# Two blocks of a transformer layer: the matrix that picks a head's decay sums written out by GpSimd, and a second add of squares

## The chip, the cores and the metric

One Trainium2 chip, one core. The time is microseconds on the device for one run of the whole program. The program's engines are TensorE (PE; its weight loads are shown apart as PEld), VectorE (DVE), ScalarE (ACT), GpSimd (POOL) and SyncE (SP), which issues the DMAs.

## The reference

Two blocks work on 256 tokens of width 1024 in float32. The first is a mixer of attention and a recurrence, then a mixture of 32 experts; each ends in a layer norm. The second, where the change lies, is a mixer with a Mamba-2 scan, then a gated MLP. Of that mixer what matters is this, cut down:

```python
u = rmsnorm(h, norm_mix_w)
gate_a, gate_s, b_a, c_a, v_a, z, xbc, dt_raw = split(u @ w_in)
y_a = (b_a * causal_dwconv(c_a * v_a, conv_a_w)) @ w_a_out
xs, bs, cs = split(silu(causal_dwconv(xbc, ssd_conv_w) + ssd_conv_b))
dt = softplus(dt_raw + dt_bias)
a_cum = cumsum(dt * -exp(a_log))
decay_in = exp(where(causal, a_cum[l] - a_cum[s], -inf))
y = (C_l . B_s * decay_in[l, s]) @ (xs * dt) + ...
yf = (y + d_skip * xs) * silu(z)
yf = yf * rsqrt(mean(yf * yf over a group of 512) + EPS) * ssd_norm_w
out = (sigmoid(gate_a) * y_a + sigmoid(gate_s) * (yf @ w_s_out)) @ w_o
```

There are 32 heads of 64 and 4 groups of 8 heads. a_cum is kept for each head and token, and each head needs its own row of 256 sums on all 128 partitions.

## The kernel before

The program is one list of instructions for each engine, in the order in which the code writes them; semaphores hold them together. `mixer2` (L1506) holds the lists of the second block's mixer: `sync`, `gpsimd`, `scalar`, `vector`, `tensor`. It follows the experts, whose last work is a layer norm of the two token tiles; that norm's last DVE instruction (L227) raises `s.h_ready` to 1 and then 2.

**Products.** Activations lie with features on partitions and 256 tokens along the row. The weights come in units of 1024x256, numbered 0 to 55. Each float32 factor is split in a high part, rounded to F32R, and a low part, so that one product becomes three (L167 to L169, high by high, low by high, high by low). A unit is 48 such products of 256 columns. For each unit SP loads 1 MB into one of three slots, ACT rounds it (L111) and DVE takes the difference (L115); TensorE runs the unit when that is done and its PSUM bank has been read.

**The start of the mixer.** When h is normed, ACT sums its squares, TensorE scales and transposes h in one step (L1947), ACT rounds the result to `u_hi` (L1658), and DVE makes `u_lo` from it (L1787, eight instructions of 256 columns, one operand in PSUM and one in SBUF). DVE's list runs L227, L115 for unit 0, L1782 (half of a norm's weights), L1784 (`w_dt_lo`, the low part of the step widths' weights, both operands in SBUF), the eight L1787, then L115 for units 1 and 2. TensorE's unit 0 waits before each group of three products for its piece of `u_lo`. After unit 0 come 24 small products with `w_dt`, then units 1, 2 and so on.

**The scan.** Units 24 to 27 also make the sums: `acum`, 64 rows by 256 tokens, holds for each of 32 heads the high part and, 32 rows below, the low part of its sums. `pick` is a matrix of 64x32 with a one at rows h and 32 + h of column h: DVE writes it (L1887) as the sum of two pieces of the identity. From unit 28 on, each unit goes with two heads: `row_sums` (L1985) multiplies a column of `pick`, read with a step of zero as a 64x128 matrix, with `acum`, which puts the head's sums on all partitions; ACT makes the decay from it, DVE weighs it (L1863), and `scan_out` (L1995, L1996) multiplies it with the tokens.

```python
out, head = s.bank[3 + p % 2][:, T * hh:T * hh + T], pick[:, h:h + 1].to_broadcast([2 * N_HEADS, P])
m = pe.matmul(out, lhsT=head, rhs=acum[:, :], start=True, stop=True)
```

**The squares.** When the four blocks of a group are done, POOL multiplies them with the gate (L1635), ACT squares them in two pieces of 128x512 (L1715), POOL adds the two (L1638) and so leaves two blocks of 256 tokens, and TensorE sums over partitions and blocks with a constant matrix (`mean_squares`, L2007, float32, two passes for each block). ACT makes the root and POOL scales (L1641). For groups 0, 1 and 2 this stands in TensorE's list behind units 35, 38 and 42, each time ahead of a `scan_out`. Group 3 has no add on POOL and takes four products.

Of the kernel before, what the change touches and what calls it, by code (L numbers as in the profile page):

```python
# [10 lines left out]
F32R = mybir.dt.float32r  # L11
# [5 lines left out]
P = 128  # L17
T = 256
# [1487 lines left out]
def mixer2(nc, A, s):  # L1506

    XBC_TAPS, A_TAPS, N_HEADS, N_GROUPS = 4, 3, 32, 4
    with ExitStack() as ctx:
        def sb(name, shape, dt=FP32):  # L1510
            return ctx.enter_context(nc.sbuf_tensor(name, shape, dt))
# [3 lines left out]
        def sem(name):  # L1515
            sems.append(nc.alloc_semaphore(name))
            return sems[-1]
# [12 lines left out]
        squares = [bcv[:, 6:8, :].rearrange("p a t -> p (a t)"), sb("squares", [P, 2 * T])[:, :]]  # L1530
# [5 lines left out]
        shift = sb("decay_shift", [P, 3, N_HEADS])  # L1536

        acum = sb("acum_hi_lo", [2 * N_HEADS, T], F32R)
        pick = sb("pick_head", [2 * N_HEADS, N_HEADS], F32R)
        rstd = sb("group_rstd", [P, T])  # L1540
        half_w = sb("half_norm_w", [P, 16])

        C = lambda name: s.con[:, SHARED.index(name), :]
# [13 lines left out]
            "cb_mm", "cbm_ready", "xt_mm", "xtok_ready", "row_mm", "decay_ready", "m_ready", "y_mm", "y_ready", "z_tanh",  # L1557
            "gated", "squared", "ms_mm", "rstd_ready", "normed", "y_hi", "y_done"))
        w_dt_split, dt_heads_mm, dt_copied = sem("m3_w_dt_split"), sem("m3_dt_heads_mm"), sem("m3_dt_copied")
        squares_added = sem("m3_squares_added")  # L1560
        merged, merged_hi, merged_done, out_first, h_done = (sem("m3_" + n) for n in (
            "merged", "merged_hi", "merged_done", "out_first", "h_done"))
        s.h_done = h_done
# [52 lines left out]
                st.load(sp, n // 3, n % 3, unit(n), 4, 512)  # L1616

        def gpsimd(pool):
            pool.wait_ge(evac_sem[2], 4)
            pool.wait_ge(evac_sem[1], 4)  # L1620
            pool.wait_ge(evac_sem[0], 4)
            for j in range(4):
                c = pair(bcv, 4 + j)
                pool.tensor_tensor(c, c, pair(bcv, 8 + j), ALU.mult).then_inc(cv_ready, 1)
            for j in range(4):
                pool.wait_ge(conv_a, j + 1)
                pool.wait_ge(cv_ready, 4)
                pool.tensor_tensor(pair(bcv, j), pair(bcv, j), pair(bcv, 8 + j), ALU.mult).then_inc(ya_ready, 1)

            for g in range(N_GROUPS):  # L1630
                y = xbc[:, 4 * g:4 * g + 4, :].rearrange("p a t -> p (a t)")
                pool.wait_ge(y_ready, 4 * g + 4)
                pool.wait_ge(evac_sem[(33 + 2 * g) % 3], use_of[33 + 2 * g] + 1)
                pool.wait_ge(evac_sem[(32 + 2 * g) % 3], use_of[32 + 2 * g] + 1)
                pool.tensor_tensor(y, y, zt[:, 4 * g:4 * g + 4, :].rearrange("p a t -> p (a t)"), ALU.mult).then_inc(gated, 1)  # L1635
                if g < N_GROUPS - 1:
                    pool.wait_ge(squared, 2 * g + 2)
                    pool.tensor_tensor(squares[0], squares[0], squares[1], ALU.add).then_inc(squares_added, 1)  # L1638
                pool.wait_ge(rstd_ready, g + 1)
                pool.wait_ge(gated, g + 1)  # L1640
                pool.tensor_tensor(xbc[:, 4 * g:4 * g + 4, :], xbc[:, 4 * g:4 * g + 4, :],  # L1641
                                   rstd[:, :].unsqueeze(1).to_broadcast([P, 4, T]), ALU.mult).then_inc(normed, 1)
# [134 lines left out]
        def vector(dve):  # L1777
            own = Count(dve, dve_own)
            step = own.add
# [99 lines left out]
            for n in range(24, 44):  # L1879
                if n == 24:  # L1880
                    ya_low(3)
                if n == 25:
                    for g in range(4):
                        masked_cb(g)
                    dve.wait_ge(shift_ready, 1)
                    lo = slice(N_HEADS, 2 * N_HEADS)
                    step(dve.tensor_tensor(pick[:, :], C("identity")[0:2 * N_HEADS, 0:N_HEADS], C("identity")[0:2 * N_HEADS, lo], ALU.add))  # L1887
                    own.wait()
                    dve.tensor_tensor(acum[lo, :], s.bank[7][lo, P:P + T], acum[lo, :].bitcast(FP32), ALU.subtract).then_inc(shift_ready, 1)
                if n in (26, 27):  # L1890
                    for f in range(4):
# [47 lines left out]
        def tensor(pe):  # L1939
# [38 lines left out]
            def row_sums(p):  # L1978

                if p >= 2:  # L1980
                    pe.wait_ge(decay_ready, p - 1)
                for hh in range(2):
                    h = 2 * p + hh
                    out, head = s.bank[3 + p % 2][:, T * hh:T * hh + T], pick[:, h:h + 1].to_broadcast([2 * N_HEADS, P])
                    m = pe.matmul(out, lhsT=head, rhs=acum[:, :], start=True, stop=True)  # L1985
                m.then_inc(row_mm, 1)

# [10 lines left out]

            def mean_squares(g):
                if g < N_GROUPS - 1:  # L2000
                    parts = 2
                    pe.wait_ge(squares_added, g + 1)
                else:
                    parts = 4
                    pe.wait_ge(squared, 2 * g + 2)
                for i in range(parts):
                    m = pe.matmul(s.bank[7][:, 0:T], lhsT=C("mean512"), rhs=squares[i // 2][:, T * (i % 2):T * (i % 2) + T], start=(i == 0), stop=(i == parts - 1))  # L2007
                m.then_inc(ms_mm, 1)
# [27 lines left out]
                        m.then_inc(xt_mm, 1)  # L2036
            pe.wait_ge(xtok_ready, 5)
            pe.wait_ge(shift_ready, 2)
            row_sums(0)
            for n in range(28, 44):  # L2040
                if n == 28:
# [422 lines left out]
```

## Time and profile before

| | |
|---|---|
| median of 3 runs | 1716.53 us (1716.46 to 1716.59) |
| span of the profiled execution | 1714.0 us; its own time is not given apart from the runs |
| PE busy | 1660.5 us (97%) |
| DVE busy | 679.2 us (40%), 1188 instructions |
| ACT busy | 576.4 us (34%) |
| POOL busy | 43.3 us (3%), 26 instructions |
| HBM | 312 GB/s over the span |

Times in the trace are microseconds from the span's start. The busy share of TensorE is a sum over stages: in the experts (about 230 to 1140 us) it also waits for weights from HBM, in the second block (from 1140 us) it mostly does not. The granted clock of TensorE has two levels, 1.0 (2.4 GHz) and 0.5 (1.2 GHz). A record's length includes the time in which the instruction stood at its engine's door, so a longer record of the same form shows a hindrance and not more work.

### The profile page before, as it was taken

How to read it: one execution, taken by the hardware profiler on the slowest of the kernel's cores; microseconds unless marked ns; L12 is line 12 of the kernel's file. 1: busy time of each engine (PE TensorE's matmuls, PEld its weight loads, DVE VectorE, ACT ScalarE, POOL GpSimd, SP SyncE). 2: the span in 40 equal slices, each digit the busy share in tenths (PEclk: the TensorE clock that was granted, in tenths of full speed). 3: DMA queues.
4: the chain of work that ended last, by engine and by line, in shares of the span. 5: the costliest groups of instructions: out<-in, count | busy, mean ns of one | idle time of the engine just before them, and what ended most of it. 6: DMA issues, size and time to landing. Idle time of an engine off the chain costs nothing.

```text
span 1714.0 us, 24055 instructions
## 1 busy us (share of the span) xinstructions
PE 1660.5 (97%) x9963; PEld 1057.6 (62%) x9963; DVE 679.2 (40%) x1188; ACT 576.4 (34%) x818; POOL 43.3 (3%) x26
## 2 busy tenths in 40 slices
PE   8999999999999999999999999999999999999998
PEld 7999863333333333333333333349999999989996
DVE  4676651212121212121212121244597565666654
ACT  5653521111111111111111111144464687465433
POOL 0000000000000000000000000000100032000000
PEclk9999999999999999999999999999999999999999
DMA  8554999999999999999999999975555444555552
GB/s 265 197 191 130 346 391 414 425 430 430 429 431 430 430 429 433 427 432 429 431 430 431 430 430 429 430 262 175 182 181 174 143 141 136 173 184 175 190 188 86
DMA packets 150860, 535.09 MB, mean 312 GB/s; under 512 B 7890, under 2 KB 102510, under 8 KB 118030
## 3 DMA queue, kind: packets, MB, share of 16 engines
q1 hardware_dynamic: 150798, 534.20, 79.3%
q8 instruction: 46, 0.75, 0.2%
q14 instruction: 16, 0.13, 0.0%
HBM read 533.13 MB, written 1.05 MB: 312 GB/s over the span
## 4 chain that ended last, share of the span: by engine, by line
PE 61%; DMA 16%; DVE 1%; ACT 1%; issue 0%; SPq 0%; ACTq 0%
PE bank L1389 15%; PE bank L167 10%; PE bank L168 10%; PE bank L169 10%; PE bank L1405 8%; DMA expert_weights_late<-in_expert_w_up_dram 8%; DMA expert_weights<-in_expert_w_up_dram 8%; PE bank L1371 2%; PE bank L1352 2%; PE bank L1396 2%; PE bank L1360 1%; PE bank L1995 0%; PE bank L1365 0%; PE bank L1985 0%; ACT back_w_hi L111 0%
## 5 line engine op out<-in xcount | busy, mean ns | idle before, releaser
L1289 DVE TENSOR_TENSOR pre_act<-bank,bias_now 128x512 f32<-128x512 f32 x64 | 44.0, 687 | 657.4 <-PE bank L1396 657.4
L115 DVE TENSOR_TENSOR back_w_lo<-raw_weights,back_w_hi 128x2048 fp32r<-128x2048 f32 x90 | 205.6, 2286 | 92.2 <-ACT back_w_hi L111 91.1
L1389 PE MATMUL bank<-expert_weights_late,x_gathered 128*64 128x512 f32 x1024 | 226.6, 594 | 15.1 <-DMA expert_weights_late<-in_expert_w_up_dram 15.1
L111 ACT ACTIVATE back_w_hi<-raw_weights 128x2048 fp32r<-128x2048 f32 x90 | 170.1, 1891 | 95.5 <-PE bank L169 95.5
L167 PE MATMUL bank<-u_hi,back_w_hi 128*128 128x256 f32 x704 | 201.0, 285 | 0.0
L168 PE MATMUL bank<-u_lo,back_w_hi 128*128 128x256 f32 x704 | 199.1, 283 | 0.0
L169 PE MATMUL bank<-u_hi,back_w_lo 128*128 128x256 f32 x704 | 199.1, 283 | 0.0
L1389 PEld LDWEIGHTS bank<-expert_weights_late,x_gathered 128*64 128x64 f32 x1024 | 72.1, 137 | 166.3 <-issue 135.1
L1389 PE MATMUL bank<-expert_weights,x_gathered 128*64 128x512 f32 x736 | 163.6, 594 | 10.0 <-DMA expert_weights<-in_expert_w_up_dram 10.0
L1211 ACT ACTIVATE raw_weights<-bank 128x512 f32<-128x512 f32 x32 | 19.1, 597 | 399.9 <-PE bank L1389 399.9
L167 PEld LDWEIGHTS bank<-u_hi,back_w_hi 128*128 128x128 f32 x704 | 134.9, 192 | 2.1 <-issue 0.4
L169 PEld LDWEIGHTS bank<-u_hi,back_w_lo 128*128 128x128 f32 x704 | 135.0, 192 | 0.0
L168 PEld LDWEIGHTS bank<-u_lo,back_w_hi 128*128 128x128 f32 x704 | 135.0, 192 | 0.0
L1389 PEld LDWEIGHTS bank<-expert_weights,x_gathered 128*64 128x64 f32 x736 | 51.9, 137 | 117.6 <-issue 96.7
L1405 PE MATMUL bank<-expert_weights_late,activations 128*64 128x512 f32 x512 | 113.4, 595 | 0.2 <-DVE activations L1302 0.2
L167 PE MATMUL bank<-v_hi,back_w_hi 128*128 128x256 f32 x352 | 99.9, 284 | 0.2 <-DVE v_lo L2214 0.2
L168 PE MATMUL bank<-v_lo,back_w_hi 128*128 128x256 f32 x352 | 99.6, 283 | 0.0
L169 PE MATMUL bank<-v_hi,back_w_lo 128*128 128x256 f32 x352 | 99.6, 283 | 0.0
L1227 ACT ACTIVATE raw_weights<-bank 128x512 f32<-128x512 f32 x32 | 19.1, 597 | 207.9 <-PE bank L1405 207.9
L1405 PE MATMUL bank<-expert_weights,activations 128*64 128x512 f32 x384 | 85.5, 594 | 0.0
L167 PE MATMUL bank<-x_hi,m_w_hi 128*128 128x256 f32 x272 | 77.7, 286 | 0.0
L168 PE MATMUL bank<-x_lo,m_w_hi 128*128 128x256 f32 x272 | 76.8, 282 | 0.0
(412 smaller groups left out, 2656.7 us busy)
## 6 DMA issues: line engine op xcount, KB each, us to landing
expert_weights_late<-in_expert_w_up_dram SPq DMA_DIRECT2D x64, 2048.0 KB, 26.3
expert_weights<-in_expert_w_up_dram SPq DMA_DIRECT2D x46, 2048.0 KB, 26.3
expert_weights_late<-in_expert_w_down_dram SPq DMA_DIRECT2D x32, 2048.0 KB, 29.5
raw_weights<-in_w_in_dram SPq DMA_DIRECT2D x56, 1024.0 KB, 5.3
expert_weights<-in_expert_w_down_dram SPq DMA_DIRECT2D x24, 2048.0 KB, 29.5
raw_weights<-in_expert_w_up_dram SPq DMA_DIRECT2D x15, 2048.0 KB, 24.2
raw_weights<-in_w_up_dram SPq DMA_DIRECT2D x22, 1024.0 KB, 5.0
raw_weights<-in_expert_w_down_dram SPq DMA_DIRECT2D x8, 2048.0 KB, 30.0
```

The lines of the kernel that those rows point to most:

```text
L111: act.activation(self.w_hi[:, s, 0:size], self.s.raw[:, s, 0:size], ACT.Copy).then_inc(self.hi_done, 1)
L115: dve.tensor_tensor(self.w_lo[:, s, 0:size], self.s.raw[:, s, 0:size], self.w_hi[:, s, 0:size].bitcast(FP32), ALU.subtract).then_inc(self. ...
L167: pe.matmul(out, lhsT=ah, rhs=bh, start=start, stop=False, skip_group_check=shared)
L168: pe.matmul(out, lhsT=ah, rhs=bl, start=False, stop=False, skip_group_check=shared)
L169: return pe.matmul(out, lhsT=al, rhs=bh, start=False, stop=stop, skip_group_check=shared)
L1211: act.activation(up_rows[:, 0, :], U[0][:, :], ACT.Copy).then_inc(up_out, 1)
L1289: dve.tensor_tensor(both.rearrange("p g k n -> p (g k) n").rearrange("p a (h n) -> p a h n", h=2), TB[b][:, :].rearrange("p (a h n) -> p a ...
L1352: m = pe.matmul(TB[0][rows[c], :], lhsT=onehot[:, t, :], rhs=s.h[:, t, 512 * c:512 * c + 512], start=(t == 0), stop=(t == 1))
L1371: m = pe.matmul(s.bank[ACC + 2 * t + c][:, :], lhsT=scatter[rows[c], P * t:P * t + P], rhs=y_rows[rows[c], :], start=False, stop=True, ski ...
L1389: m = pe.matmul(U[b][rows[half], :], lhsT=xg[:, 2 * u + a, :], rhs=w[:, a, 512 * c:512 * c + 512], start=(first and a == 0), stop=(last an ...
L1396: m = pe.transpose(TB[b][:, P * gk:P * gk + P], up_rows[:, b, gk:512:4], C("identity"))
L1405: m = pe.matmul(U[0][rows[c], :], lhsT=act_t[:, b, g, half, :], rhs=w[:, half, g, 512 * c:512 * c + 512], start=(b + half + g == 0), stop= ...
```

## The change

`pick` becomes 64x32x128, written out: 4096 numbers on each of 64 partitions. POOL writes it with one add of two pieces of the identity, each read with a step of zero along the last axis, as its first instruction in the mixer, as soon as h is normed (`h_ready` = 2). DVE's small add and the wait behind it are gone. TensorE waits once for `pick_ready` before the first row sums, and reads a plain 64x128 matrix.

In groups 0 to 2 POOL adds, behind its add of the two pieces, the second block of 256 tokens to the first, having waited for its own add; TensorE then takes one product in place of two, and waits for the second add.

```diff
@@ -1536,7 +1536,7 @@
         shift = sb("decay_shift", [P, 3, N_HEADS])
 
         acum = sb("acum_hi_lo", [2 * N_HEADS, T], F32R)
-        pick = sb("pick_head", [2 * N_HEADS, N_HEADS], F32R)
+        pick = sb("pick_head", [2 * N_HEADS, N_HEADS, P], F32R)
         rstd = sb("group_rstd", [P, T])
         half_w = sb("half_norm_w", [P, 16])
 
@@ -1557,7 +1557,7 @@
             "cb_mm", "cbm_ready", "xt_mm", "xtok_ready", "row_mm", "decay_ready", "m_ready", "y_mm", "y_ready", "z_tanh",
             "gated", "squared", "ms_mm", "rstd_ready", "normed", "y_hi", "y_done"))
         w_dt_split, dt_heads_mm, dt_copied = sem("m3_w_dt_split"), sem("m3_dt_heads_mm"), sem("m3_dt_copied")
-        squares_added = sem("m3_squares_added")
+        squares_added, pick_ready = sem("m3_squares_added"), sem("m3_pick_ready")
         merged, merged_hi, merged_done, out_first, h_done = (sem("m3_" + n) for n in (
             "merged", "merged_hi", "merged_done", "out_first", "h_done"))
         s.h_done = h_done
@@ -1616,6 +1616,9 @@
                 st.load(sp, n // 3, n % 3, unit(n), 4, 512)
 
         def gpsimd(pool):
+            head_of = lambda c: C("identity")[0:2 * N_HEADS, c:c + N_HEADS].unsqueeze(2).to_broadcast([2 * N_HEADS, N_HEADS, P])
+            pool.wait_ge(s.h_ready, 2)
+            pool.tensor_tensor(pick[:, :, :], head_of(0), head_of(N_HEADS), ALU.add).then_inc(pick_ready, 1)
             pool.wait_ge(evac_sem[2], 4)
             pool.wait_ge(evac_sem[1], 4)
             pool.wait_ge(evac_sem[0], 4)
@@ -1636,6 +1639,8 @@
                 if g < N_GROUPS - 1:
                     pool.wait_ge(squared, 2 * g + 2)
                     pool.tensor_tensor(squares[0], squares[0], squares[1], ALU.add).then_inc(squares_added, 1)
+                    pool.wait_ge(squares_added, 2 * g + 1)
+                    pool.tensor_tensor(squares[0][:, 0:T], squares[0][:, 0:T], squares[0][:, T:2 * T], ALU.add).then_inc(squares_added, 1)
                 pool.wait_ge(rstd_ready, g + 1)
                 pool.wait_ge(gated, g + 1)
                 pool.tensor_tensor(xbc[:, 4 * g:4 * g + 4, :], xbc[:, 4 * g:4 * g + 4, :],
@@ -1884,8 +1889,6 @@
                         masked_cb(g)
                     dve.wait_ge(shift_ready, 1)
                     lo = slice(N_HEADS, 2 * N_HEADS)
-                    step(dve.tensor_tensor(pick[:, :], C("identity")[0:2 * N_HEADS, 0:N_HEADS], C("identity")[0:2 * N_HEADS, lo], ALU.add))
-                    own.wait()
                     dve.tensor_tensor(acum[lo, :], s.bank[7][lo, P:P + T], acum[lo, :].bitcast(FP32), ALU.subtract).then_inc(shift_ready, 1)
                 if n in (26, 27):
                     for f in range(4):
@@ -1981,7 +1984,7 @@
                     pe.wait_ge(decay_ready, p - 1)
                 for hh in range(2):
                     h = 2 * p + hh
-                    out, head = s.bank[3 + p % 2][:, T * hh:T * hh + T], pick[:, h:h + 1].to_broadcast([2 * N_HEADS, P])
+                    out, head = s.bank[3 + p % 2][:, T * hh:T * hh + T], pick[:, h, :]
                     m = pe.matmul(out, lhsT=head, rhs=acum[:, :], start=True, stop=True)
                 m.then_inc(row_mm, 1)
 
@@ -1998,8 +2001,8 @@
 
             def mean_squares(g):
                 if g < N_GROUPS - 1:
-                    parts = 2
-                    pe.wait_ge(squares_added, g + 1)
+                    parts = 1
+                    pe.wait_ge(squares_added, 2 * g + 2)
                 else:
                     parts = 4
                     pe.wait_ge(squared, 2 * g + 2)
@@ -2036,6 +2039,7 @@
                         m.then_inc(xt_mm, 1)
             pe.wait_ge(xtok_ready, 5)
             pe.wait_ge(shift_ready, 2)
+            pe.wait_ge(pick_ready, 1)
             row_sums(0)
             for n in range(28, 44):
                 if n == 28:
```

On POOL, from the last instruction of the first block to the first group, before; `b_c_v` holds the convolutions' inputs and later the squares, `x_b_c` the scan's output:

```order
L433 MEMSET expert_weights 128x1024
L2377 UNCONDITIONAL_BRANCH
L2403 ISA
L2418 UNCONDITIONAL_BRANCH
L1624 ISA
L1624 TENSOR_TENSOR b_c_v<-b_c_v 128x512 x4
L1628 TENSOR_TENSOR b_c_v<-b_c_v 128x512 x4
L1635 TENSOR_TENSOR x_b_c<-x_b_c,z 128x1024
L1638 TENSOR_TENSOR b_c_v<-b_c_v,squares 128x512
L1641 TENSOR_TENSOR x_b_c<-x_b_c,group_rstd 128x1024
```

and now:

```order
L433 MEMSET expert_weights 128x1024
L2381 UNCONDITIONAL_BRANCH
L2407 ISA
L2422 UNCONDITIONAL_BRANCH
L1621 ISA
L1621 TENSOR_TENSOR pick_head<-shared_constants 64x4096
L1627 TENSOR_TENSOR b_c_v<-b_c_v 128x512 x4
L1631 TENSOR_TENSOR b_c_v<-b_c_v 128x512 x4
L1638 TENSOR_TENSOR x_b_c<-x_b_c,z 128x1024
L1641 TENSOR_TENSOR b_c_v<-b_c_v,squares 128x512
L1643 TENSOR_TENSOR b_c_v<-b_c_v 128x256
L1646 TENSOR_TENSOR x_b_c<-x_b_c,group_rstd 128x1024
```

Two instructions are new: the add of 64x4096 ahead of everything else of this mixer, and one add of 128x256 in each of groups 0 to 2.

On DVE, at the place of the old add, before:

```order
L1850 TENSOR_TENSOR x_b_c<-bank,shared_constants 128x128
L1887 TENSOR_TENSOR pick_head<-shared_constants 64x32
L1889 TENSOR_TENSOR acum_hi_lo<-bank,acum_hi_lo 32x256
L115 TENSOR_TENSOR back_w_lo<-raw_weights,back_w_hi 128x2048
L1856 TENSOR_TENSOR b_c_v<-bank,dt 128x512 x4
```

and now:

```order
L1855 TENSOR_TENSOR x_b_c<-bank,shared_constants 128x128
L1892 TENSOR_TENSOR acum_hi_lo<-bank,acum_hi_lo 32x256
L115 TENSOR_TENSOR back_w_lo<-raw_weights,back_w_hi 128x2048
L1861 TENSOR_TENSOR b_c_v<-bank,dt 128x512 x4
```

The small add is gone and nothing else on DVE moves; its list at the mixer's start is as before.

## Rows read from the trace of the kernel before

**Rows 1.** Stretches, core 0: us, busy time of each engine, granted clock, DMA.

```profile
1151.00:1154.40 3.40, 3.40 (x19) 3.40 (x18) 1.61 (x4) 1.97 (x7) 0.00 (x0) 0.50 0.38 86
...
1169.00:1399.00 230.00, 230.00 (x1893) 223.51 (x1892) 155.62 (x190) 137.48 (x195) 22.55 (x12) 1.00 0.54 165
```

**Rows 2.** Timeline of DVE, mixer's start: start us, length, line, tiles, [idle before].

```profile
1148.32 1.28 DVE L227 SCALAR_TENSOR_TENSOR hidden<-hidden,expert_weights_top 128x1024 f32<-128x1024 f32 x1
1149.53 2.28 DVE L115 TENSOR_TENSOR back_w_lo<-raw_weights,back_w_hi 128x2048 fp32r<-128x2048 f32 x1
1151.73 0.17 DVE L1782 TENSOR_SCALAR half_norm_w<-parameter_cols 128x16 f32<-128x16 f32 x1
1151.81 0.42 DVE L1784 TENSOR_TENSOR w_dt_lo<-w_dt,w_dt_hi 128x256 fp32r<-128x256 f32 x1
1154.01 3.29 DVE L1787 SCALAR_TENSOR_TENSOR u_lo<-bank,parameter_cols,u_hi 128x256 fp32r<-128x256 f32 x8 [1.79 <-ACT u_hi L1658]
1157.22 4.48 DVE L115 TENSOR_TENSOR back_w_lo<-raw_weights,back_w_hi 128x2048 fp32r<-128x2048 f32 x2
```

**Rows 3.** Timeline of TensorE over the same stretch.

```profile
1149.66 5.47 PE L1947 MATMUL bank<-group_rstd,hidden 128*128 128x128 f32 x32 [2.10 <-DVE hidden L227]
1154.89 0.36 PE L167 MATMUL bank<-u_hi,back_w_hi 128*128 128x256 f32 x1
...
1157.48 0.28 PE L167 MATMUL bank<-u_hi,back_w_hi 128*128 128x256 f32 x1
1157.60 0.28 PE L168 MATMUL bank<-u_lo,back_w_hi 128*128 128x256 f32 x1
```

**Rows 4.** Timelines of POOL and DVE, 1371 to 1376 us.

```profile
1371.21 2.41 POOL L1635 TENSOR_TENSOR x_b_c<-x_b_c,z 128x1024 f32<-128x1024 f32 x1 [76.17 <-DVE z L1907]
...
1372.18 3.58 DVE L115 TENSOR_TENSOR back_w_lo<-raw_weights,back_w_hi 128x2048 fp32r<-128x2048 f32 x1 [1.11 <-ACT back_w_hi L111]
```

**Rows 5.** Timelines of DVE and POOL, 1379 to 1384 us.

```profile
1379.37 2.29 DVE L115 TENSOR_TENSOR back_w_lo<-raw_weights,back_w_hi 128x2048 fp32r<-128x2048 f32 x1 [1.11 <-ACT back_w_hi L111]
1381.58 2.05 DVE L1863 TENSOR_TENSOR b_c_v<-b_c_v,x_b_c 128x768 f32<-128x768 f32 x1
...
1380.45 2.36 POOL L1638 TENSOR_TENSOR b_c_v<-b_c_v,squares 128x512 f32<-128x512 f32 x1 [6.83 <-ACT squares L1715]
```

**Rows 6.** POOL's products by line: ns min/median/max, first and last start, form.

```profile
L1628 POOL TENSOR_TENSOR b_c_v<-b_c_v x4: 1293/1296/1297, 1241.8 to 1293.7; 128x512 f32<-128x512 f32 x4
...
L1635 POOL TENSOR_TENSOR x_b_c<-x_b_c,z x4: 2380/2392/2408, 1371.2 to 1449.4; 128x1024 f32<-128x1024 f32 x4
```

**Rows 7.** The same view: weight loads of L1985 and L889, DVE's L1887.

```profile
L1985 PEld LDWEIGHTS bank<-acum_hi_lo,pick_head x32: 182/184/186, 1327.2 to 1430.2; 64*128 64x128 f32 x32
...
L889 PEld LDWEIGHTS bank<-expert_weights x16: 187/187/187, 36.5 to 67.2; 64*128 64x128 f32 x16
...
L1887 DVE TENSOR_TENSOR pick_head<-shared_constants x1: 174/174/174, 1314.7 to 1314.7; 64x32 fp32r<-64x32 f32 x1
```

**Rows 8.** Chain of waits, 1327 to 1445 us: start us, us, what.

```profile
1327.23 0.66 PE bank L1985 x4
...
1334.64 0.43 PE bank L1985 x2
1335.07 0.32 PE bank L167
...
1384.08 0.86 PE bank L2007 x4
...
1444.96 0.32 PE bank L167
```

**Rows 9.** Timelines of POOL, DVE and TensorE at group 1's squares.

```profile
1402.85 2.37 POOL L1638 TENSOR_TENSOR b_c_v<-b_c_v,squares 128x512 f32<-128x512 f32 x1 [8.54 <-ACT squares L1715]
...
1403.98 2.71 DVE L1876 SCALAR_TENSOR_TENSOR ya_lo<-x_b_c,half_norm_w,ya_hi 128x256 fp32r<-128x256 f32 x4
...
1407.61 0.44 PE L1995 MATMUL bank<-b_c_v 128*64 128x256 f32 x2 [0.27 <-DVE b_c_v L1863]
```

## The prediction

> **What bounds the kernel now.** I read the stretches first, then the timelines of DVE, PE and POOL around the two places that the diff touches, then the chain of waits. Through the mixer's body TensorE is busy in every microsecond: 230.00 of 230.00 us at full clock, with POOL at 22.55 us [rows 1]. So from about 1169 us on, a microsecond added to or taken from TensorE's queue is one of the whole time. The mixer's start is different. It is a chain through DVE: the second L227 (the norm of h, which raises h_ready to 2) starts at 1148.32 and takes 1.28 us; behind it on DVE stand L115, L1782, L1784 and the eight L1787 that make u_lo [rows 2]. TensorE scales and transposes h in L1947 until about 1155.1 and starts unit 0 at 1154.89; its eighth group of three products, which needs the eighth u_lo, starts at 1157.48, and that u_lo was finished at 1154.01 + 3.29 = 1157.30 [rows 2, 3]. So DVE is only 0.2 us ahead of TensorE there. Anything that holds DVE between L115 and L1787 for longer than the 1.79 us that DVE now waits for u_hi is on the path.
>
> **Part one, the written-out pick: what it costs on POOL and DVE.** POOL gets one add of 64x4096, released by h_ready = 2, so at 1148.32 + 1.28 = 1149.6. Its length is not in the trace. POOL's products of 512 elements a partition take 1.296 us and those of 1024 take 2.392 [rows 6], so 1.096 us for 512 more (2.14 ns each) and 0.2 fixed; 4096 give 0.2 + 8.75 = 8.95 us. Bounds: half of it (4.5), if reading with a step of zero were one read for many elements, and double (17.9), if rounding to F32R cost a second pass; both are guesses around these rows, and I take 8.95, as L1641's broadcast operand and the plain operands run through the same loop.
>
> Where it runs decides. DVE and POOL do not work beside each other when both read two operands from SBUF. At 1371.21 POOL takes 2.41 us, to 1373.62; an L115 issued at 1372.18 ends at 1375.76, which is 3.58 us instead of 2.29, and 2.14 us after POOL's end: it stood still until POOL was through [rows 4, 5]. The other way round, L1638, issued at 1380.45 while an L115 ran to 1381.66, ends 1.15 us after that, so its own 1.30 less 0.15 of start-up; and the next DVE instruction, L1863, in line from 1381.58, had to wait for POOL again (2.05 us, to 1383.63) [rows 5]. So a POOL instruction that already waits goes ahead of DVE's next one. Whether a DVE instruction with one operand in PSUM is held too, these rows don't tell; it stands in DVE's queue either way.
>
> At the start this reads so. DVE's L115 starts at 1149.53, just ahead of h_ready, and ends at 1151.81 [rows 2]. POOL waits for it and then goes ahead of L1784, the subtraction for w_dt_lo with both operands in SBUF: POOL ends at 1151.81 + 8.95 - 0.15 = 1160.6. L1784 ends 0.3 later, at 1160.9. The eight L1787 are behind it, and all u_hi are long there: 3.29 us, the last ending at 1164.1 instead of 1157.30. That is 6.8 us later; TensorE had 0.2 us in hand, and loses some 0.1 in starting after a stop (an estimate between 0 and the 0.2 that the first L167 after a stop has over 0.12 on the chain [rows 8]): **+6.7 us** on TensorE. The other work behind it is covered: the two L115 for units 1 and 2 [rows 2] would end near 1166 and 1169, and those units start after all of unit 0 and w_dt's products.
>
> The rows show POOL holding DVE for whole instructions of 1.3 and 2.4 us; none is longer, and I take it that 9 us are held as a whole too.
> The Trainium skill (SBUF — State Buffer, "SBUF: two separate sides") calls the shared port pair an exclusive lock that is kept for the whole instruction by whichever starts first, and the 3.58 us row agrees. By it a 9 us instruction holds DVE for 9 us, and the sum is the one above; by the rows alone a hold could also end after the 2.4 us that they show, u_lo would start some 0.4 us late, and this part of the sum would be +0.3.
>
> **The clock.** TensorE would stand from 1155.1 to about 1161.5, 6.4 us. In this stage an idle of 2.10 us before L1947 was followed by 3.40 us at a granted clock of 0.50, which is 1.2 instead of 2.4 GHz [rows 1, 3]. I expect the same after a longer idle. At full clock a product of unit 0 starts every 0.12 us [rows 3]; at half clock I estimate twice that, 0.24. In 3.4 us 14 products are done instead of the 25 that u_lo's pace allows (3.29/8 = 0.41 us for three): 11 x 0.12 = **+1.3 us**. Bounds: 0, if the low stretch falls into the idle, and 2.9 if two such stretches come.
>
> **The written-out pick on TensorE: 0.** The weight loads with the zero step take 184 ns (L1985) and those of L889, 64x128 without it, 187 [rows 7]. On the chain the first four row sums take 0.66 us and a pair alone 0.43, so the second pair costs 0.23, or 0.115 each, the 0.12 of a plain F32R product. What a pair has beyond that, 0.2, is at the change of the tile's shape from 128x64 to 64x128, and the same 0.32 us stand at the first L167 whether it follows row sums (1335.07) or L1996 (1444.96) [rows 8]. The shape stays 64x128. Bounds: 0 and 16 x 0.2 = 3.2 us of gain.
>
> DVE loses its own pick add, L1887, 174 ns at 1314.7; the row sums start at 1327.2 [rows 7], so 12 us of other work hide it: 0. The new wait for pick_ready on TensorE is met some 160 us before it.
>
> **Part two, the squares.** For groups 0 to 2 TensorE drops one of two FP32 products, each two passes: 0.86 us becomes 0.43 [rows 8], at most 3 x 0.43 = 1.3 us gained. POOL adds a 128x256 add, 0.2 + 0.55 = 0.75 us, behind its own L1638, and it meets the same lock. Group 0: L1638 ends at 1382.81, the held L1863 goes first (to 1383.63) [rows 5], the new add ends near 1384.2, and the one product ends near 1384.8 instead of 1384.08 + 0.86 = 1384.94 [rows 8]: -0.1. Group 2 has the same neighbours: -0.1. Group 1: L1638 ends at 1405.22 with four L1876 queued on DVE since 1403.98, both of whose operands are in SBUF; the new add gets in after the first of them and puts 0.5 us into DVE's queue, and TensorE already waits for DVE there (0.27 us before L1995) [rows 9]: +0.5, and the 0.43 saved ends in the wait. Sum **+0.3**; bounds -1.3 and +1.5 (0.5 for each group).
>
> **Sum**: 6.7 + 1.3 + 0 + 0.3 = +8.3 us. The profiled execution has a span of 1714.0, and the median of the runs is 1716.53; the 2.5 us around the span are not touched, so 1716.53 + 8.3 = **1724.8 us**.
>
> **Rivals.**
> 1. *The hold misses the path* (not slower). L1784 slips in ahead of POOL, or POOL lets go early, or an operand with step zero does not need the port. Then POOL lies under the u_lo instructions, if their one operand in PSUM keeps them free, and holds only the L115 of units 1 and 2, which have some 4 us to spare. For it: L1784 is in DVE's queue when L115 ends. Against it: L1863 was in the queue too and came second [rows 5], and between L115 and L1784 stands L1782, which gives POOL 0.1 us more [rows 2]. Time: +0.3, so 1716.8. It decides where L1784 starts before POOL's add.
> 2. *The add is slower than POOL's products*, up to 17.9 us. Then 8.9 more: 1733.7. For it: 64x4096 with F32R out is a form that no row shows.
> 3. *The zero step does cost TensorE*: the row sums lose their 0.2 each, the squares save their whole 1.3, and the hold misses the path: 1716.53 - 3.2 - 1.3 = 1712.0. Against it stand the equal weight loads and the equal pace [rows 7, 8].
>
> **How the numbers follow.** Forecast 0.70, rival 1 0.15, rival 2 0.12, rival 3 0.03. The range takes the forecast and rival 2: its lower end is a POOL add of half the length (4.4 us less, 1720.4) with the clock's share gone too, 1719; its upper end is the double length, 1734. A measurement of this kernel tells some 0.2%, 3.4 us, from no change. Slower by more: forecast and rival 2, 0.82, as all but the lowest microsecond of the range lies above 1719.9. Within it: rival 1, 0.15. Faster by more: rival 3, 0.03.
>
> **What would show it.** In the changed profile: a POOL add of about 9 us from 1151.7 to 1160.6; the subtraction for w_dt_lo taking about 9 us where it took 0.42; TensorE idle some 6.4 us before unit 0 with u_lo as the releaser; a low clock after it; row sums at 0.43 a pair as now; L2007 with half its records and a wait before it or before L1995. Wrong, if w_dt_lo ends before 1153, if POOL's add is far from 9 us, or if a pair of row sums falls to 0.24.

## The result and the profile after

The change makes the kernel slower: 1723.98 us median of 5 runs (1723.15 to 1724.16) against 1716.53 us (5 runs, 1715.42 to 1717.21). The ratio is 1.0044, with a 95% interval of 1.0033 to 1.0054, so +7.45 us, where +8.3 was forecast. The span of the profiled execution is 1722.0 us, against 1714.0.

In the changed kernel the line numbers of the mixer are 3 to 5 higher: L1784 (w_dt_lo) is L1789, L1787 (u_lo) is L1792, L1947 is L1950; L1782 (half_norm_w) is L1787. The timelines of DVE and POOL at the mixer's start, which answer to [rows 2] (start us, length us, engine, line, operation, tiles, idle before):

```profile
1149.61 1.29 DVE L227 SCALAR_TENSOR_TENSOR hidden<-hidden,expert_weights_top 128x1024 f32<-128x1024 f32 x1
1150.81 2.28 DVE L115 TENSOR_TENSOR back_w_lo<-raw_weights,back_w_hi 128x2048 fp32r<-128x2048 f32 x1
1153.01 7.00 DVE L1787 TENSOR_SCALAR half_norm_w<-parameter_cols 128x16 f32<-128x16 f32 x1
1159.92 0.41 DVE L1789 TENSOR_TENSOR w_dt_lo<-w_dt,w_dt_hi 128x256 fp32r<-128x256 f32 x1
1160.26 3.21 DVE L1792 SCALAR_TENSOR_TENSOR u_lo<-bank,parameter_cols,u_hi 128x256 fp32r<-128x256 f32 x8
...
1150.98 9.00 POOL L1621 TENSOR_TENSOR pick_head<-shared_constants 64x4096 fp32r<-64x4096 f32 x1 [1054.21 <-DVE hidden L227]
```

POOL's add ends at 1159.98. The 16 columns of half_norm_w, 0.17 us before, take 7.00 and end with it; w_dt_lo and u_lo, both of their old length, stand behind. TensorE shows the wait ([rows 3] before):

```profile
1150.95 5.47 PE L1950 MATMUL bank<-group_rstd,hidden 128*128 128x128 f32 x32 [2.10 <-DVE hidden L227]
1160.88 0.35 PE L167 MATMUL bank<-u_hi,back_w_hi 128*128 128x256 f32 x1 [4.46 <-DVE u_lo L1792]
...
1162.33 0.41 PE L167 MATMUL bank<-u_hi,back_w_hi 128*128 128x256 f32 x1
1162.55 0.41 PE L168 MATMUL bank<-u_lo,back_w_hi 128*128 128x256 f32 x1
```

Unit 0's products first start 0.12 us apart, then 0.21. The stretches (busy us of PE, PEld, DVE, ACT, POOL, granted clock, DMA share, GB/s) show the clock there, as [rows 1] did:

```profile
1151.00:1154.40 3.40, 3.40 (x18) 3.40 (x19) 3.40 (x2) 1.98 (x5) 3.40 (x1) 0.56 0.09 14
1161.60:1165.00 3.40, 3.40 (x18) 3.40 (x18) 3.40 (x6) 0.00 (x0) 0.00 (x0) 0.51 0.00 0
1165.00:1167.00 2.00, 2.00 (x19) 2.00 (x19) 2.00 (x2) 0.00 (x0) 0.00 (x0) 0.98 0.11 13
```

Where the profiled 8.0 us come from can be read by comparing the starts of the same instructions in the two traces. L227 ends at 1150.90 instead of 1149.61, so 1.29 us are there before the changed code begins. In the eleven experiments below, in none of which the work that leads to it is changed, this end lies 0.2 us earlier to 2.2 us later than in the profiled execution of before: it varies by itself, and experiments 4 and 10, which have the same written-out pick, are level with the kernel before. From there on: unit 0 starts +4.71 us late, the products of w_dt that follow it another +1.48, and then nothing for 170 us: the first row sums start 7.47 us late, as w_dt did. The scan adds 0.52: +0.49 at group 1, -0.11 at group 2, +0.03 at group 0, and some 0.1 spread over the steps. So 6.7 us of the trace belong to the change.

The chain of waits, which answers to [rows 8] (start us, us, what):

```profile
1153.10 6.91 DVE half_norm_w L1787
...
1334.70 0.67 PE bank L1988 x4
...
1342.12 0.43 PE bank L1988 x2
1342.56 0.32 PE bank L167
...
1390.43 1.34 POOL b_c_v L1643
1391.81 0.70 PE bank L2010 x2
...
1411.64 3.11 DVE ya_lo L1881 x4
...
1444.67 0.70 PE bank L2010 x2
```

The row sums take the same 0.67, 0.43 and 0.32. The squares' product at groups 0 and 2 takes 0.70 instead of 0.86, where 0.43 was forecast. From its start to the start of `scan_out` behind it 0.63 us pass instead of 0.95, so 0.32 is saved; but it starts later, by 0.35 us at group 0, where TensorE waits for POOL's second add (L1643), and by 0.21 at group 2. At group 1 the chain runs through DVE.

### The profile page after: what moved, and what is told of

It reads as the page before. It is cut to its first block, busy times and chain, and to the rows that moved or that the text cites. A ratio compares the mean times of both kernels' runs of the same rounds, so it can differ in the third digit from the quotient of the medians.

```text
span 1722.0 us, 24046 instructions
## 1 busy us (share of the span) xinstructions
PE 1661.9 (97%) x9957; PEld 1058.2 (61%) x9957; DVE 686.4 (40%) x1187; ACT 576.3 (33%) x818; POOL 55.8 (3%) x30
## 4 chain that ended last, share of the span: by engine, by line
PE 60%; DMA 16%; DVE 2%; ACT 1%; issue 1%; POOL 0%; SPq 0%; ACTq 0%; POOLq 0%
PE bank L1389 14%; PE bank L167 10%; PE bank L169 9%; PE bank L168 9%; PE bank L1405 8%; DMA expert_weights_late<-in_expert_w_up_dram 8%; DMA expert_weights<-in_expert_w_up_dram 8%; PE bank L1371 2%; PE bank L1352 2%; PE bank L1396 2%; PE bank L1360 1%; PE bank L1998 0%; PE bank L1365 0%; DVE half_norm_w L1787 0%; DVE back_w_lo L115 0%
## 5 line engine op out<-in xcount | busy, mean ns | idle before, releaser
L115 DVE TENSOR_TENSOR back_w_lo<-raw_weights,back_w_hi 128x2048 fp32r<-128x2048 f32 x90 | 205.6, 2287 | 91.6 <-ACT back_w_hi L111 90.6
```

Of the source, the lines that this page charges most:

```text
L115: dve.tensor_tensor(self.w_lo[:, s, 0:size], self.s.raw[:, s, 0:size], self.w_hi[:, s, 0:size].bitcast(FP32), ALU.subtract).then_inc(self. ...
```

## The experiments

The theory after the result: POOL's add waited for L115's instruction (2.0 of its 9.0 us), then ran 7.0 us and held DVE's next instruction; the clock and group 1 add the rest. The rivals: the 9.0 us are all work beside L115; the squares carry a good part; it is the written-out pick itself; only half_norm_w's form contends. One number sums up the mixer's start: the time from L227's end to the first product of w_dt, worked out from each trace, 11.11 us before and 17.30 after.

**1. Part one alone** (the second add of squares left out, two products on TensorE as before).

```diff
-                    pool.wait_ge(squares_added, 2 * g + 1)
-                    pool.tensor_tensor(squares[0][:, 0:T], squares[0][:, 0:T], squares[0][:, T:2 * T], ALU.add).then_inc(squares_added, 1)
-                    parts = 1
-                    pe.wait_ge(squares_added, 2 * g + 2)
+                    parts = 2
+                    pe.wait_ge(squares_added, g + 1)
```

> Part one alone: the pick is written out by GpSimd, the squares are summed as before. Theory (the hold at the start of the mixer makes nearly all of the loss): unit 0 starts 4.7 us later than before, the column pass of w_dt another 1.5 us later, nothing is added at groups 0, 1 and 2; the time is about 0.4 us under that of the change, 1723.5 us, and at least 6 us over the kernel before. Rival (the squares carry a good part of the loss): under 1721 us.

Measured: 1723.92 us, ratio 1.0044 (1.0027 to 1.0061). Unit 0 +4.71, as expected; the scan adds 0.11 us in all. The step to w_dt is 2.64, not 1.5. The timeline of TensorE:

```profile
1150.79 4.23 PE L1948 MATMUL bank<-group_rstd,hidden 128*128 128x128 f32 x32 [2.10 <-DVE hidden L227]
1160.72 0.55 PE L167 MATMUL bank<-u_hi,back_w_hi 128*128 128x256 f32 x1 [5.70 <-DVE u_lo L1790]
```

and its stretches:

```profile
1151.00:1154.40 3.40, 3.27 (x28) 3.08 (x28) 3.40 (x2) 2.50 (x7) 3.40 (x1) 1.00 0.14 18
1161.60:1165.00 3.40, 3.40 (x18) 3.40 (x18) 3.40 (x6) 0.00 (x0) 0.00 (x0) 0.50 0.00 0
1165.00:1167.00 2.00, 2.00 (x12) 2.00 (x12) 2.00 (x2) 0.00 (x0) 0.00 (x0) 0.56 0.25 24
```

In this execution the clock did not fall behind the 2.1 us of idle ahead of the transposes, which took 4.23 instead of 5.47 us; the gain ended in the wait for u_lo. It fell behind the longer idle, from unit 0's first product, and stayed low past 1165. So which idle the fall follows differs from one execution to the next; the loss at the start of the mixer is 6.2 us in the trace of the change and 7.3 in this one, both against the trace of before, whose transposes were slow. Against an execution in which they ran at full clock as they did here (experiment 2, whose start of the mixer is that of before), it is 8.0 us here: unit 0 starts 9.99 us behind L227's end instead of 4.48, so +5.5, and the step to w_dt is another 2.5. Like compared with like, the loss there is 6.2 or 8.0 us.

**2. Part two alone**, the same lines added to the kernel before.

> Part two alone, on the kernel before: GpSimd folds a group's squares to one block, the pick is read with a step of zero as before. Theory: the start of the mixer is as before, the scan gains 0.4 us in all: 0 at group 0, +0.5 at group 1, where the new add lies beside VectorE's ya_lo and TensorE waits for VectorE, -0.1 at group 2; about 1716.9 us. Rival (the squares carry a good part of the loss): over 1719 us.

Measured: 1716.75 us, ratio 1.0001 (0.9992 to 1.0011). Group 0 +0.03, group 1 +0.49, group 2 -0.13; the mixer's start takes 10.47 us, with transposes of 4.23. The squares cost 0.4 us by the trace, too little to be seen in the times, and the loss is part one's. TensorE at the mixer's start:

```profile
1150.20 4.23 PE L1949 MATMUL bank<-group_rstd,hidden 128*128 128x128 f32 x32 [2.10 <-DVE hidden L227]
1154.63 0.35 PE L167 MATMUL bank<-u_hi,back_w_hi 128*128 128x256 f32 x1 [0.20 <-DVE u_lo L1789]
```

**3. The same pick, written later.**

```diff
-            pool.wait_ge(s.h_ready, 2)
+            pool.wait_ge(st.lo_done, 3)
             pool.tensor_tensor(pick[:, :, :], head_of(0), head_of(N_HEADS), ALU.add).then_inc(pick_ready, 1)
```

> The pick add waits until VectorE has written the three low parts of h, when VectorE has some 9 us without work of its own; all else as in the change. Theory (the loss is the hold of VectorE's half_norm_w and of the u_lo behind it): unit 0 and w_dt start as in the kernel before, within 0.2 us, and 0.4 us of the squares stay: about 1716.9 us. The add's length tells the two readings of its 9.0 us apart: 9.0 us again if that was work beside L115's instruction, about 6.9 us if 2.1 us of it were a wait for that instruction's end. Rival (the loss hangs on the written-out pick itself, wherever it is written): within 2 us of the change, 1722 to 1726 us.

Measured: 1717.75 us, ratio 1.0008 (0.9998 to 1.0017); the mixer's start takes 11.29 us. POOL's timeline:

```profile
1164.16 7.02 POOL L1621 TENSOR_TENSOR pick_head<-shared_constants 64x4096 fp32r<-64x4096 f32 x1 [1066.80 <-DVE back_w_lo L115]
```

All but some 0.7 us of the loss is gone in the trace (0.18 at the mixer's start, 0.49 in the scan), and the times are not told from those before, with the same add and the same row sums. The add takes 7.02 us where DVE is free. In the changed kernel 9.00 - 7.02 = 1.98 us of its record were a wait: it began at about 1153.0, where L115 ended (1153.09).

**4. Late, and group 1 as before** (the second add only for groups 0 and 2), on top of the late pick.

```diff
+                    if g == 1:
+                        pool.wait_ge(squares_added, 3)
+                    else:
+                        pool.wait_ge(squares_added, 1 + 3 * (g // 2))
+                        pool.tensor_tensor(squares[0][:, 0:T], squares[0][:, 0:T], squares[0][:, T:2 * T], ALU.add).then_inc(squares_added, 1)
...
+                    parts = 2 if g == 1 else 1
+                    pe.wait_ge(squares_added, (2, 3, 5)[g])
```

> As the late pick, and group 1 alone keeps two blocks of squares for TensorE, while groups 0 and 2 are folded by GpSimd. Theory (the new add of group 1 stands between VectorE's ya_lo, which TensorE waits for): the +0.5 us at group 1 goes and the -0.1 us at group 2 stays: 0.5 us under the late pick, about 1716.4 us, level with the kernel before. Rival (group 1's loss came from elsewhere on VectorE's queue): the marker of group 1 stays 0.5 us late.

Measured: 1716.43 us, ratio 1.0001 (0.9991 to 1.0011); group 1 +0.00, group 2 -0.11. DVE at group 1, first in the change, where it takes 0.5 us longer (2.71 before, [rows 9]):

```profile
1411.55 3.20 DVE L1881 SCALAR_TENSOR_TENSOR ya_lo<-x_b_c,half_norm_w,ya_hi 128x256 fp32r<-128x256 f32 x4
```

and here:

```profile
1403.23 2.71 DVE L1884 SCALAR_TENSOR_TENSOR ya_lo<-x_b_c,half_norm_w,ya_hi 128x256 fp32r<-128x256 f32 x4
```

**5. half_norm_w moved behind the u_lo and the next low parts**, so that w_dt_lo comes first behind L115.

```diff
             split_lo(dve, 0)
-            step(dve.tensor_scalar(half_w[:, :], s.colrange("ssd_norm_w_2", 0, 16), 0.5, None, op0=ALU.mult))
             dve.wait_ge(w_dt_split, 1)
...
+            step(dve.tensor_scalar(half_w[:, :], s.colrange("ssd_norm_w_2", 0, 16), 0.5, None, op0=ALU.mult))
             dve.wait_ge(dt_mm, 1)
```

> half_norm_w (one 128x16 operand of one-operand form) moves from ahead of w_dt_lo to behind the low parts of h; w_dt_lo is then VectorE's first instruction behind L115's. Theory A (whatever VectorE starts next while GpSimd's pick add runs is held to its end): w_dt_lo takes about 6.5 us instead of 0.4, u_lo ends as in the change, unit 0 starts 4.5 us later than before, the time is within 0.5 us of the change. Theory B (the one-operand form alone contends with GpSimd, two SBUF operands go beside it as L115's do): w_dt_lo takes under 1 us, unit 0 starts within 0.3 us of the kernel before.

Measured: 1723.99 us (one run); unit 0 +4.63. Theory A, by DVE's timeline:

```profile
1152.92 7.25 DVE L1788 TENSOR_TENSOR w_dt_lo<-w_dt,w_dt_hi 128x256 fp32r<-128x256 f32 x1
```

**6. Both moved behind the u_lo.**

```diff
             split_lo(dve, 0)
-            step(dve.tensor_scalar(half_w[:, :], s.colrange("ssd_norm_w_2", 0, 16), 0.5, None, op0=ALU.mult))
-            dve.wait_ge(w_dt_split, 1)
-            dve.tensor_tensor(w_dt_lo[:, :, :], w_dt[:, :, :], w_dt_hi[:, :, :].bitcast(FP32), ALU.subtract).then_inc(w_dt_split, 1)
             for k in range(KD):
...
+            step(dve.tensor_scalar(half_w[:, :], s.colrange("ssd_norm_w_2", 0, 16), 0.5, None, op0=ALU.mult))
+            dve.wait_ge(w_dt_split, 1)
+            dve.tensor_tensor(w_dt_lo[:, :, :], w_dt[:, :, :], w_dt_hi[:, :, :].bitcast(FP32), ALU.subtract).then_inc(w_dt_split, 1)
```

> half_norm_w and w_dt_lo both move behind the eight u_lo, so that u_lo (one operand in PSUM, one in SBUF) come first behind L115's instruction, while GpSimd's pick add runs. Theory A (every VectorE instruction that starts beside the add is held): the first u_lo is held to the add's end, some 6.8 us, and unit 0 starts some 4 us later than before. Theory B (an operand in PSUM, or any form but half_norm_w's, isn't held): u_lo end by 1157 us in the trace's time, unit 0 starts within 0.3 us of before, w_dt_lo is written at about 1160.4 us, 1 us ahead of its first use, and 4.5 us and the clock's 1.5 us are saved.

Measured: 1718.34 us (one run); unit 0 +0.44, the mixer's start 11.70 us. The timelines of DVE and POOL:

```profile
1150.53 2.28 DVE L115 TENSOR_TENSOR back_w_lo<-raw_weights,back_w_hi 128x2048 fp32r<-128x2048 f32 x1
1155.70 3.23 DVE L1789 SCALAR_TENSOR_TENSOR u_lo<-bank,parameter_cols,u_hi 128x256 fp32r<-128x256 f32 x8 [2.89 <-ACT u_hi L1663]
1158.85 0.88 DVE L1791 TENSOR_SCALAR half_norm_w<-parameter_cols 128x16 f32<-128x16 f32 x1
1159.64 0.41 DVE L1793 TENSOR_TENSOR w_dt_lo<-w_dt,w_dt_hi 128x256 fp32r<-128x256 f32 x1
...
1150.69 9.00 POOL L1621 TENSOR_TENSOR pick_head<-shared_constants 64x4096 fp32r<-64x4096 f32 x1 [1054.26 <-DVE hidden L227]
```

Theory B: while POOL's add runs, to 1159.69, the eight u_lo with one operand in PSUM take 3.23 us, as without it, and the half_norm_w behind them is held to the add's end. They ended at 1158.93, not by 1157, and unit 0 came 0.44 us late, not within 0.3, because they waited for u_hi, not for POOL. Another order of the same DVE instructions takes some 5.6 us off the mixer's start (17.30 to 11.70), with POOL's add where the change put it.

**7. Fillers ahead of unit 0** (five products of constants into a bank that nothing reads).

```diff
+            for i in range(5):
+                pe.matmul(s.bank[1][:, :], lhsT=C("identity"), rhs=s.con[:, 1:5, :].rearrange("p n c -> p (n c)"), start=True, stop=True)
             u, ya = (u_hi, u_lo), (ya_hi, ya_lo)
```

> Five products of the identity with the constants go ahead of unit 0, on TensorE alone, into a bank that nothing reads. Theory (the second 1.5 us of the loss is the clock, which falls to half behind the 4.5 us in which TensorE has no work): the fillers take some 1 to 2 us of that gap, the granted clock over the first 3.4 us of unit 0 reads 1.0 or above half, w_dt starts only 4.7 us later than before and not 6.2, and the time is 1 to 1.5 us under the change. Rival (the step from unit 0 to w_dt is something else, or the remaining gap of some 2.5 us suffices for the fall): the step stays 1.5 us.

Measured: 1722.66 us, 1.3 under the change; one run doesn't tell that much (the change's five runs lie within 1.0 us, 25 runs of the kernel before within 3.1), the trace does. Unit 0 +4.71, then +0.14. The timeline of TensorE, and the stretch of unit 0's beginning:

```profile
1154.83 4.46 PE L1965 MATMUL bank<-shared_constants 128*128 128x512 f32 x10
1160.70 0.36 PE L167 MATMUL bank<-u_hi,back_w_hi 128*128 128x256 f32 x1 [1.41 <-DVE u_lo L1792]
```

```profile
1161.60:1165.00 3.40, 3.40 (x30) 3.40 (x29) 3.40 (x6) 0.00 (x0) 0.00 (x0) 1.00 0.00 0
```

With an idle of 1.41 us instead of 4.46 the clock stayed at 1.00. The second step of the loss was the clock: 1.48 - 0.14 = 1.3 us against the trace of the change, and 2.64 - 0.14 = 2.5 against experiment 1, whose transposes also ran at full clock, as here.

**8. A plain add in the place of the pick's, the pick late.**

```diff
             pool.wait_ge(s.h_ready, 2)
+            plain = s.h[0:2 * N_HEADS, :, :].rearrange("p t d -> p (t d)")
+            pool.tensor_tensor(pick[:, 0:16, :].rearrange("p h c -> p (h c)"), plain, plain, ALU.add).then_inc(pick_ready, 1)
+            pool.wait_ge(st.lo_done, 3)
```

> At the start of the mixer GpSimd adds two plain operands (h to itself, 64 partitions x 2048, no step of zero) into part of pick's place, and writes the real pick late as in the late pick; the first is extra work whose result is overwritten. Theory A (the step of zero decides whether an add on GpSimd takes part in the contention): the plain add waits for the end of L115's instruction and so shows 2.1 + some 4.4 us from 1151.0 us, or starts at 1153.1. Theory B (every add of GpSimd goes beside L115's): it starts at once and takes some 4.4 us, half_norm_w is held from 1153.0 to 1155.4, unit 0 starts about on time. The late pick takes 9.0 us if that was its own length, 6.9 if it had waited.

Measured: 1719.19 us (one run); unit 0 +1.28. The timelines of DVE and POOL:

```profile
1153.15 3.57 DVE L1791 TENSOR_SCALAR half_norm_w<-parameter_cols 128x16 f32<-128x16 f32 x1
...
1151.11 5.58 POOL L1622 TENSOR_TENSOR pick_head<-hidden 64x2048 fp32r<-64x2048 f32 x1 [1054.31 <-DVE hidden L227]
1164.66 7.02 POOL L1625 TENSOR_TENSOR pick_head<-shared_constants 64x4096 fp32r<-64x4096 f32 x1 [7.98 <-DVE back_w_lo L115]
```

Neither theory's numbers: it waited (2 us, to L115's end) and then took 3.6 us, not 4.4. That it waits with plain operands too agrees with A's first half and shows that the step of zero does not decide who waits; a record that begins at once is no sign that the work does. Half the elements, half the hold.

**9. Lengths of POOL's adds**, all results overwritten later, in the time after u_lo in which DVE is free.

```diff
             pool.wait_ge(st.lo_done, 3)
+            flat = s.con[:, 1:5, :].rearrange("p n c -> p (n c)")
+            pool.tensor_tensor(squares[1], flat, flat, ALU.mult).then_inc(pick_ready, 1)
+            pool.wait_ge(pick_ready, 1)
+            pool.tensor_tensor(squares[1], flat, flat, ALU.add).then_inc(pick_ready, 1)
...
```

> Ahead of the late pick add GpSimd runs five small ones on constants, while VectorE has no work: 128x512 multiplied, 128x512 added, 64x512 added, 64x512 added with a step of zero, 64x512 added into the F32R tile. They are extra work, overwritten later. They tell why the pick add took 7.02 us, 1.7 ns an element, where the products of the kernel before gave 2.1. Theory A (an add is faster than a product): the product takes 1.3 us, all adds about 1.05. Theory B (64 partitions are faster than 128): the two on 128 partitions take 1.3 us, the three on 64 about 1.05. Theory C (the length is a fixed part and a smaller rate: 512 elements take 1.3 us in any form, and 4096 take 7.02, so 1.6 ns each and 0.5 us): all five take 1.3 us. The step of zero and the F32R output change nothing in any of the three.

Measured, in the order of the text, by POOL's timeline:

```profile
1161.90 1.04 POOL L1624 TENSOR_TENSOR squares<-shared_constants 128x512 f32<-128x512 f32 x1 [1064.78 <-DVE back_w_lo L115]
1163.02 1.04 POOL L1626 TENSOR_TENSOR squares<-shared_constants 128x512 f32<-128x512 f32 x1
1164.14 1.03 POOL L1628 TENSOR_TENSOR squares<-shared_constants 64x512 f32<-64x512 f32 x1
1165.25 1.03 POOL L1630 TENSOR_TENSOR squares<-shared_constants 64x512 f32<-64x512 f32 x1
1166.36 1.03 POOL L1632 TENSOR_TENSOR pick_head<-shared_constants 64x512 fp32r<-64x512 f32 x1
1167.47 7.02 POOL L1634 TENSOR_TENSOR pick_head<-shared_constants 64x4096 fp32r<-64x4096 f32 x1
```

None of the three theories: all five take 1.03 to 1.04, product or sum, 64 or 128 partitions, with or without the step of zero, F32 or F32R. (7.02 - 1.03) / 3584 = 1.67 ns an element and 0.18 fixed, where [rows 6] had given 2.14 and 0.2. What differs from the kernel's own products was still open. The pick, which starts 5.7 us behind the end of DVE's L115 here and 0.1 us behind it in experiment 3, met DVE's next work on two operands in SBUF (DVE's timeline):

```profile
1170.97 3.60 DVE L1814 SCALAR_TENSOR_TENSOR dt<-dt,dt_tmp 128x64 f32<-128x64 f32 x1 [1.02 <-ACT dt_tmp L1688]
```

0.23 us without it; the L115 behind it came 1.5 us late and TensorE waited 1.46 us for it (1718.19 us, one run). The place of experiment 3 has 7.9 us in it, for an add of 7.0.

**10. The late pick with eight fillers instead of six** ahead of the transposes, group 1 as before.

```diff
-            for i in range(6):
+            for i in range(8):
                 pe.matmul(s.bank[1][:, :], lhsT=C("identity"), rhs=s.con[:, 1:5, :].rearrange("p n c -> p (n c)"), start=True, stop=True)
             pe.wait_ge(s.h_ready, 2)
```

> The late pick with group 1 left as before, and eight instead of six filler products ahead of the scaling and transposing of h, so that TensorE's idle of 2.1 us there shrinks to some 0.3 us. Theory (in some executions the clock falls behind that idle and the transposes take 5.47 instead of 4.23 us; in others it doesn't): they take 4.23 us, at a granted clock of 1.0, and unit 0 starts 4.5 us behind h_ready rather than 5.3; the time is 0 to 0.8 us under that of the same kernel without the two fillers, 1715.6 to 1716.4 us, and not told from the kernel before. Rival (the fillers end too late and hold the transposes): slower by up to 1 us.

Measured: 1716.40 us, ratio 0.9997 (0.9988 to 1.0006): not told from the kernel before. The idle is 0.38 us and the transposes take 4.23 (timeline of TensorE):

```profile
1150.21 4.23 PE L1953 MATMUL bank<-group_rstd,hidden 128*128 128x128 f32 x32 [0.38 <-DVE hidden L227]
```

But they took 4.23 or 4.24 in experiments 1, 2, 4, 7, 9 and 11 too, without more fillers there; one profile doesn't show that the fillers prevent the fall.

**11. Operands**: five products of 128x512 in the same place: h by itself, h by another part of h, h by the constants, and twice in place.

```diff
+            pool.tensor_tensor(squares[1], h0, h0, ALU.mult).then_inc(pick_ready, 1)
+            pool.wait_ge(pick_ready, 1)
+            pool.tensor_tensor(squares[1], h0, h1, ALU.mult).then_inc(pick_ready, 1)
...
```

> Five products of 128x512 on GpSimd, whose results are overwritten, ahead of the late pick add, while VectorE has no work: h by itself, h by another part of h, h by the constants, and twice in place (the output is the first operand, then the second), as the kernel's own products are, which take 1.296 us where a product of constants by themselves took 1.04. Theory A (working in place costs the 0.26): the first three 1.04, the last two 1.3. Theory B (two operands in different places cost it): the first 1.04, the others 1.3. Theory C (neither, it comes from what runs beside the kernel's own products): all five 1.04.

Measured: 1719.27 us (one run; the pick comes later still than in experiment 9, and TensorE waits 2.48 us for DVE). By POOL's timeline (the fifth product took 1.30 too):

```profile
1161.94 1.04 POOL L1623 TENSOR_TENSOR squares<-hidden 128x512 f32<-128x512 f32 x1 [1064.54 <-DVE back_w_lo L115]
1163.06 1.29 POOL L1625 TENSOR_TENSOR squares<-hidden 128x512 f32<-128x512 f32 x1
1164.43 1.29 POOL L1627 TENSOR_TENSOR squares<-hidden,shared_constants 128x512 f32<-128x512 f32 x1
1165.80 1.30 POOL L1629 TENSOR_TENSOR squares<-squares,shared_constants 128x512 f32<-128x512 f32 x1
```

Theory B: a tile by itself takes 1.04, two operands from different places 1.29 to 1.30, in place or not. The pick add, whose two operands are columns of the identity 32 apart, each read 128 times over, runs at the faster rate; whether that is due to their nearness or to the repeated reads was not tried.

## Why the prediction was right, point by point

- **The hold at the start, +6.7: the mechanism right, the size not.** Measured +4.71. POOL did wait for L115, then went ahead of DVE's next instruction and held it for the whole of its own, and u_lo behind it was what TensorE waited for. The mis-sized term is the add's length, 8.95 us by the 2.14 ns of [rows 6]. It is 7.02: the products of [rows 6] are at the slower rate that two operands from different places show (1.29 against 1.04 us, experiments 9 and 11), the pick, which reads near columns over and over, at the faster one. 6.7 - 1.9 = 4.8, nearly as measured. By experiment 3 the loss goes when the add is moved, by experiment 6 when both instructions that may be held stand behind u_lo; with only half_norm_w moved (experiment 5) it stays. The working started from a trace with slow transposes; where they run at full clock, unit 0 can start 0.8 us earlier, and the hold takes that too (+5.5).
- **The sign that was foretold was the wrong instruction.** The prediction named the subtraction for w_dt_lo as the one held and took half_norm_w, one operand and 0.17 us, to slip through. half_norm_w was held 7.00 us; put behind, w_dt_lo is held 7.25 (experiment 5). For the sum it makes no difference. That the record of POOL's add would begin at L115's end was wrong too: it begins at its issue, and 1.98 us of it are waiting. So the sign of "a POOL add of about 9 us" was met by luck: 2 us of waiting and 7 of work.
- **Whether u_lo, with an operand in PSUM, is held** was left open. It is not: 3.23 us beside the add (experiment 6). The Trainium skill (SBUF — State Buffer, "Who interferes with whom") says that a VectorE instruction with at most one SBUF input contends with GpSimd only in the modes that use both ports, and that tensor_scalar can enter these. By that rule u_lo is free and half_norm_w, from SBUF to SBUF, may be held; the rows agree on both, the second at 7.00 us.
- **The clock, +1.3**, within bounds 0 to 2.9: 1.48 in the trace of the change, 2.64 in experiment 1, gone with fillers (experiment 7). The working (low for as long as after the earlier idle) fitted the first case, though its two counts were both too low: 18 products in the 3.4 us where it had 14 (0.21 us apart, not 0.24), and 30 at full clock, in experiment 7, where it had 25. The difference, 12 against 11, came out. In the second case the clock stayed low longer.
- **The row sums, 0.** The chain has them at the same lengths. By the scan of experiment 1, which has the written-out pick and the old squares, it adds 0.11 us in all, where experiment 2, with the old pick, has 0.00 up to group 0: not a gain, and a sliver of a loss that was not foretold and whose cause is open.
- **The squares, +0.3**: 0.4 (experiment 2). Group 1's +0.49 came by the wait that was named, POOL's second add among the four ya_lo, and goes with it (experiment 4). Group 2's -0.1 came as forecast; group 0's did not, +0.03. There POOL's second add ended about where it was forecast, but the one product behind it takes longer than half of the two (0.32 saved, not 0.43).
- **The rivals.** The first (the hold misses the path) fell, though a late pick or another order of DVE would have made it come true. The second (a slower add) fell the other way: the add was faster. The third fell with the unchanged row sums.
- The sum by the measured terms is 4.7 + 1.5 + 0.1 + 0.4 = 6.7 with slow transposes and 5.5 + 2.5 + 0.1 + 0.4 = 8.5 with fast ones, and the medians differ by 7.45, between the two. That the forecast of 8.3 is so near is in part luck: the hold was put too high by the length of the add, and the clock, and where the transposes are fast what unit 0 loses besides, came out higher than forecast.

## What to carry to other kernels

Before giving GpSimd a long elementwise instruction, look at what VectorE has next at that moment: a 0.17 us instruction behind which the critical path stands can cost the whole length of GpSimd's. Put it into a stretch in which VectorE is idle for as long as it runs, or let VectorE's PSUM-reading instructions go first. And read a length from a row with the same kind of operands: here the nearest row differed by a fifth.

## What the runs showed of the hardware

- A GpSimd add takes 1.67 ns an element with both operands the same tile, or near columns read with a step of zero, and the kernel's products of two tiles 2.14 (1.04 against 1.29 us at 128x512); 64 or 128 partitions make no difference.
- A GpSimd instruction whose record starts beside a two-operand VectorE instruction need not be running: 9.00 us on record, 7.02 of work.
- The granted clock fell behind an idle of 2.10 us in some executions and not in others (transposes of 5.47 or 4.23 us), and in the one that skipped it there, it fell behind the next, longer idle and stayed low longer.
